# Ten of eleven FFN up products a block as seven half-size block products (Strassen form) in an fp32 two-block decoder kernel

## The chip, the cores and the metric

One Trainium2 chip (trn2), one of its cores. The metric is the device time of one execution in microseconds. All data and all matmuls are fp32.

## The reference, cut to what matters

Two blocks over x of 256 tokens x 1024 features: an mLSTM layer, a conv FFN, a shared key/value projection, an attention layer, a second conv FFN; then two more layers (convolution and sparse attention) that are modulated by vectors computed from `c_2` and `w_ada_2`. The change is in the conv FFN, which runs twice:

```python
def conv_ffn(x, norm_g, w_up, conv_w, conv_b, w_down):   # x 256 x 1024, w_up 1024 x 5632, w_down 2816 x 1024
    u = rmsnorm(x, norm_g) @ w_up
    up = jnp.pad(u, ((0, 0), (CONV_W - 1, 0), (0, 0)))
    c = conv_b + up[:, 0:s_] * conv_w[0]                 # CONV_W = 3 taps over the tokens
    for j in range(1, CONV_W):
        c = c + up[:, j:j + s_] * conv_w[j]
    val, gate = jnp.split(c, 2, axis=-1)
    return (jax.nn.silu(gate) * val) @ w_down
```

## The kernel before, in words

Everything is written out by hand for five engines, which meet through counting semaphores: `eng.wait_ge(S(name), n)` holds an engine, `.then_inc(S(name), n)` raises the count when the instruction is done. Each engine's instructions run in the order in which they stand, and so do the DMAs that SyncE (SP) issues.

The activations live transposed, features on the partitions: `hT`, `xg` and `sq` are 128 x 8 x 256 (8 chunks of 128 features, 256 tokens). A weight tile is 1 MB, 128 x 8 x 256: 256 output columns for all 1024 inputs. Outside the FFN such tiles go through `ring`, eight slots, with tile n in slot n % 8; SP's `load(n)` waits until the product that last used the slot is done.

An FFN (`ffn(f)` on each engine, f = 0 and 1) takes D_FF = 2816 in 11 steps of 256 value and 256 gate columns; g = 11 f + i counts the steps over both. Steps 0, 1 and 10 are written out, steps 2 to 9 are a hardware loop of four turns of two. `fring` has two buffers (par = parity of the step), each with the value and the gate tile of w_up and the tile of w_down.

- TensorE (`up`, L958 to L971; `down`, L973 to L986): up is 2 halves (value, gate) x 2 column chunks x 8 inner chunks = 32 matmuls of 128 x 128 weights against 256 tokens. An fp32 matmul is two MATMUL instructions in the trace, each with a weight load. The product goes to banks 4 and 5 or 6 and 7 by parity. The order is up(g), down(g - 1), up(g + 1), and so on. down is 16 matmuls that accumulate into banks 0 to 3 over all steps. up(g) waits for the copies of step g - 2, down(g) for `act_ready` of step g. In the block's first product the matmuls follow `xg_ready` chunk by chunk; the matmul that sums the squares for the norm (`ss`, L814) stands after it. xg is x times the norm's gain; the factor 1/rms is applied to the product, in the copy.
- VectorE (`step`, L1461): copies the product out of PSUM times 1/rms (L1464, two of 512 elements), adds taps 1 and 2 (L1478, eight of 256), in steps 2 to 9 folds one row chunk of w_ada into an accumulator in two halves of 1536 elements (L1493), and multiplies the gated value (L1500). The first tap waits for ScalarE's tap 0.
- ScalarE (L542 to L554): tap 0 with the bias (L549, four of 256), then silu (L553).
- SP (`ffn_loads`, L329): for each step of the loop first `load_ffn`, which issues the two w_up tiles (L313, after `up_done` of step g - 2), then the w_down tile (L317, after `down_done` of step g - 2), then `load_ada` with the two halves of w_ada (L325), each of which waits for `ada_free`, raised by the fold (L1493) of that half in the step before. `f_ada` has one buffer a half:

```python
sp.wait_ge(S("ada_free"), 2 * (8 * l + k) + half + 1)      # k = i - 2
```

So SP's order in the loop is: up g, down g, w_ada of g, up g + 1, down g + 1, w_ada of g + 1. Before and after the FFN's loads stand the ring loads: 8 to 23 ahead of the first FFN, 24 to 39 ahead of the second, and after the second the bias rows (L356, `skew`).

Ahead of each FFN stand four products (tiles 12 to 15, and 28 to 31) whose results VectorE adds to hT (`add_pair`, L1324).

Of the kernel before, what the change touches and what calls it, by code (L numbers as in the profile page):

```python
# [18 lines left out]
ALU = mybir.AluOpType  # L19
ACT = mybir.ActivationFunctionType  # L20
# [99 lines left out]
def model(nc, I, out):  # L120
    with ExitStack() as ctx:
# [31 lines left out]
        def W(a, b):  # L153
            return work[:, a:b]
# [46 lines left out]
        f_t = [three(W(7168 + 512 * i, 7680 + 512 * i), 2) for i in range(2)]  # L201
        f_u = W(8192, 8192 + 4 * 258).rearrange("p (g c t) -> p g c t", g=2, c=2)
        f_sg = W(9300, 9812)

        sqf = sq[:, :, :].rearrange("p a b -> p (a b)")
        sc_sb = [sqf[:, DIAG * i:DIAG * (i + 1)] for i in range(2)]
# [37 lines left out]
        def cut(w, c, n=256):  # L244

            return w.rearrange("(k p) n -> p k n", p=P)[:, :, c:c + n]

        def slot(n):
            return ring[:, n % RING, :]

        def slot8(n):
            return slot(n).rearrange("p (k n) -> p k n", k=8)
# [24 lines left out]
        ring_count = []  # L277
        for n, parts in enumerate(loads):
            landed[n % RING] += 16 * len(parts)
            ring_count.append(landed[n % RING])  # L280

        def arrived(eng, n):

            eng.wait_ge(S(f"ring{n % RING}"), ring_count[n])

        def product(eng, n):

            eng.wait_ge(S("product"), n + 1)
# [8 lines left out]
        @block.sync  # L297
        def _(sp):
            def load(n):
                if n >= RING:  # L300
                    product(sp, n - RING)
                for dst, src in loads[n]:
                    sp.dma_start(dst, src).then_inc(S(f"ring{n % RING}"), 16)

            def load_ffn(f, i, par, first):

# [47 lines left out]
            sp.wait_ge(S("rows_out"), 16)  # L354

# [36 lines left out]
        def _(act):  # L392
# [146 lines left out]


            def ffn(f):
                def step(g, i, par):  # L542
# [12 lines left out]

                g0 = FF_STEPS * f
                for i in (0, 1):
                    step(g0 + i, i, (g0 + i) % 2)
# [226 lines left out]
        def _(pe):  # L785
# [168 lines left out]
            def ffn(f, nth):  # L954

                g0 = FF_STEPS * f

                def up(g, par, turn, x_ready=None):  # L958

                    if x_ready is None:  # L960
                        pe.wait_ge(S("u_ready"), g - 1)
                    pe.wait_ge(S(f"f_up{par}"), 32 * turn)
                    for j in range(2):
                        w = fring[:, par, j, :].rearrange("p (k n) -> p k n", k=8)
                        for c in range(2):
                            for k in range(DC):
                                if x_ready is not None and j == 0 and c == 0:
                                    x_ready(k)
                                last = mm(pb[4 + 2 * par + j][:, T * c:T * (c + 1)], w[:, k, P * c:P * (c + 1)],  # L969
                                          xg[:, k, :], start=(k == 0), stop=(k == DC - 1))  # L970
                    last.then_inc(S("up_done"), 1)  # L971

                def down(g, par, turn, first=False, end=False):  # L973

                    pe.wait_ge(S(f"f_down{par}"), 16 * turn)
                    pe.wait_ge(S("act_ready"), g + 1)
                    w = fring[:, par, 2, :].rearrange("p (k n) -> p k n", k=2)
                    for k in range(2):
                        for m in range(DC):
                            last = mm(pb[m // 2][:, T * (m % 2):T * (m % 2 + 1)], w[:, k, P * m:P * (m + 1)],  # L980
                                      f_act[:, par, T * k:T * (k + 1)],
                                      start=(first and k == 0 and m % 2 == 0), stop=(end and k == 1),
                                      skip_group_check=True)
                            if end and k == 1 and m in (1, 3, 5):
                                last.then_inc(S("out_bank"), 1)
                    last.then_inc(S("down_done"), 1)  # L986

                p = g0 % 2
                up(g0, p, g0 // 2 + 1, x_ready=xg_ready(8 + 16 * f))
                ss(nth, pb[0][:, 0:T])  # L990
                up(g0 + 1, 1 - p, (g0 + 1) // 2 + 1, x_ready=lambda k: None)
                down(g0, p, g0 // 2 + 1, first=True)
                with pe.Fori(0, 4) as j:
                    for s in range(2):
                        g = 2 * j + (g0 + s + 2)
                        up(g, (g0 + s) % 2, j + ((g0 + s) // 2 + 2))
                        down(g - 1, (g0 + s + 1) % 2, j + ((g0 + s - 1) // 2 + 2))
                g = g0 + FF_STEPS - 1
                up(g, g % 2, g // 2 + 1)
# [263 lines left out]
        def _(dve):  # L1263
# [159 lines left out]
            for h in range(M_HEADS):  # L1423
# [31 lines left out]
            def ffn(f, nth, nn):  # L1455
                residual_norm(nth)
                g0 = FF_STEPS * f
                mean_square(nth, pb[0][:, 0:T], ms[:, 0:T], D)
                newton(nn, ms[:, 0:T], rbc, nwt[:, 0:T])

                def step(g, i, par, ada=None):  # L1461
                    dve.wait_ge(S("up_done"), g + 1)
                    for q in range(2):
                        ins = v.tensor_tensor(f_u[:, q, :, 2:2 + T], three(pb[4 + 2 * par + q][:, :], 2), rbc2,  # L1464
                                              ALU.mult)
                    ins.then_inc(S("u_ready"), 1)
                    dve.wait_ge(S("u_ready"), g + 1)
                    for tap in (1, 2):
                        marks = [] if tap == 1 else marks
# [40 lines left out]
                for i in (0, 1):  # L1510
                    step(g0 + i, i, (g0 + i) % 2)
                start = done[1]
                with dve.Fori(0, 4) as j:
                    per = 2 * 7
                    done[0] = per * j
                    for s in range(2):
                        i = 2 * j + s + 2
                        step(g0 + i, i, (g0 + s) % 2, ada=16 * (2 * j + s + 1))
                    assert done[1] - start == per
                done[0], done[1] = 0, start + 4 * per  # L1520
                i = FF_STEPS - 1
# [275 lines left out]
```

## Time and profile before

| | |
|---|---|
| median of 3 runs | 1095.95 us (1094.37 to 1096.34) |
| profiled execution, first to last instruction | 1092.9 us |
| mean granted TensorE clock | 0.987 |
| TensorE (PE) matmul busy | 1031.6 us, 94% |
| TensorE weight loads (PEld) busy | 886.1 us, 81% |
| VectorE (DVE) busy | 499.7 us, 46% |
| ScalarE (ACT) busy | 251.7 us, 23% |
| DMA | 168.12 MB, mean 154 GB/s |

The profile gives for the profiled execution its span, 1092.9 us; no further time of that execution is shown, so the runs' median stands beside it, 3.0 us higher. Times in the views count from the span's start. The first FFN runs from 156.6 to about 389 us, the second from 520.2 to about 752 us. Busy shares are averages over stages with different limits; in the FFN TensorE has no gap. The granted clock is a share of full speed (2.4 GHz); 0.5 is 1.2 GHz.

### The profile page before, as it was taken

The numbers are of one execution on the slowest core, as the hardware profiler recorded it, in microseconds if no ns is written. First come the engines' busy times: TensorE is split into PE (matmuls) and PEld (weight loads), VectorE is DVE, ScalarE is ACT, GpSimd is POOL, SyncE is SP. The second block draws the span as 40 slices with busy tenths as digits, with TensorE's granted clock in tenths as the row PEclk, the third lists the DMA queues.
The fourth block names the chain that finished last, engine by engine and source line by source line (L and its number), as shares of the span: only waits on it lengthen the run. The fifth ranks groups of instructions, "written<-read, shape, count | busy, mean of one in ns | idle before, by whom it ended". The sixth has DMA issues, their size and how long they took to land.

```text
span 1092.9 us, 12810 instructions
## 1 busy us (share of the span) xinstructions
PE 1031.6 (94%) x4887; PEld 886.1 (81%) x4887; DVE 499.7 (46%) x1160; ACT 251.7 (23%) x524; POOL 17.1 (2%) x23
## 2 busy tenths in 40 slices
PE   6999899999999999999999999998998896998987
PEld 5787688888888888888888888886886685887776
DVE  2301525334533543331435335336199944189951
ACT  1111202101101112351111011014223523233432
POOL 0000000000000000000000000000002000002000
PEclk9999999999999999999999999998999998999999
DMA  8993242676676454423346765732332054323001
GB/s 259 359 326 97 63 149 77 236 248 208 223 253 214 152 195 154 146 74 119 116 174 213 254 224 198 255 104 68 118 116 78 2 171 157 118 87 106 1 1 39
DMA packets 128832, 168.12 MB, mean 154 GB/s; under 512 B 7555, under 2 KB 116115, under 8 KB 128659
## 3 DMA queue, kind: packets, MB, share of 16 engines
q1 hardware_dynamic: 124592, 164.70, 45.6%
q10 hardware_dynamic: 4195, 2.81, 0.9%
q8 instruction: 29, 0.48, 0.2%
q14 instruction: 16, 0.13, 0.0%
HBM read 166.31 MB, written 1.06 MB: 153 GB/s over the span
## 4 chain that ended last, share of the span: by engine, by line
PE 77%; DVE 19%; ACT 2%; issue 1%; DMA 0%; ACTq 0%; DVEq 0%
PE bank L969 28%; PE bank L796 15%; PE bank L980 14%; DVE work L1657 8%; PE bank L807 8%; PE bank L1213 4%; PE bank L1127 1%; DVE fring L1679 1%; DVE sq L1594 1%; DVE fring L1692 1%; PE bank L1089 1%; PE bank L1245 1%; DVE fring L1688 1%; DVE sq L1585 1%; PE bank L814 1%
## 5 line engine op out<-in xcount | busy, mean ns | idle before, releaser
L969 PE MATMUL bank<-xg,fring 128*128 128x256 f32 x1408 | 307.6, 379 | 1.1 <-DVE xg L1307 1.1
L969 PEld LDWEIGHTS bank<-xg,fring 128*128 128x128 f32 x1408 | 267.4, 190 | 37.8 <-issue 1.5
L796 PE MATMUL bank<-xg,ring 128*128 128x256 f32 x960 | 218.5, 387 | 11.2 <-ACT xg L670 8.2
L796 PEld LDWEIGHTS bank<-xg,ring 128*128 128x128 f32 x960 | 185.3, 194 | 41.6 <-issue 9.9
L980 PE MATMUL bank<-work,fring 128*128 128x256 f32 x704 | 155.6, 379 | 0.0
L980 PEld LDWEIGHTS bank<-work,fring 128*128 128x128 f32 x704 | 133.4, 190 | 18.3 <-issue 0.3
L549 ACT ACTIVATE work<-work,cols 128x256 f32<-128x256 f32 x88 | 45.8, 592 | 291.2 <-DVE work L1464 291.2
L1464 DVE TENSOR_TENSOR work<-bank,rstd 128x512 f32<-128x512 f32 x44 | 28.4, 686 | 174.5 <-PE bank L969 174.5
L1657 DVE SCALAR_TENSOR_TENSOR work<-work,cols 128x256 f32<-128x256 f32 x240 | 98.5, 484 | 1.4 <-ACT work L709 1.3
L1478 DVE SCALAR_TENSOR_TENSOR work<-work,cols 128x256 f32<-128x256 f32 x176 | 71.6, 480 | 53.3 <-ACT work L549 53.3
L807 PE MATMUL bank<-ring,xg 128*128 128x256 f32 x320 | 69.9, 379 | 0.0
L807 PEld LDWEIGHTS bank<-ring,xg 128*128 128x128 f32 x320 | 60.6, 190 | 8.1
L1213 PE MATMUL bank<-ring,fring 128*128 128x256 f32 x256 | 57.1, 380 | 2.1 <-DVE fring L1720 2.1
L1493 DVE SCALAR_TENSOR_TENSOR work<-work,cact 128x1536 f32<-128x1536 f32 x32 | 58.1, 1816 | 0.6
L796 PE MATMUL bank<-work,ring 128*128 128x256 f32 x256 | 56.2, 379 | 0.5 <-ACT work L636 0.5
L1213 PEld LDWEIGHTS bank<-ring,fring 128*128 128x128 f32 x256 | 48.3, 190 | 10.0 <-issue 2.9
L796 PEld LDWEIGHTS bank<-work,ring 128*128 128x128 f32 x256 | 48.4, 190 | 7.1 <-ACT work L636 0.7
L1324 DVE TENSOR_TENSOR hT<-hT,bank 128x512 f32<-128x512 f32 x16 | 11.0, 687 | 58.1 <-PE bank L796 51.6
L622 ACT ACTIVATE sq<-sq,sml 128x128 f32<-128x128 f32 (+1 forms) x48 | 21.5, 449 | 46.7 <-DVE sml L1585 46.7
L406 ACT ACT_TABLE_LOAD x21 | 26.9, 1283 | 22.4 <-issue 22.0
L387 POOL TENSOR_TENSOR fring<-fring 128x384 f32<-128x384 f32 x16 | 16.1, 1012 | 1005.3 <-DVE fring L1696 959.4
L442 ACT ACTIVATE sq<-hT 128x512 f32<-128x512 f32 x24 | 14.8, 630 | 73.3 <-DVE hT L1324 68.8
(231 smaller groups left out, 761.5 us busy)
## 6 DMA issues: line engine op xcount, KB each, us to landing
fring<-in_f_w_up SPq DMA_DIRECT2D x44, 1024.0 KB, 10.2
work<-in_w_ada SPq DMA_DIRECT2D x32, 768.0 KB, 6.0
fring<-in_f_w_down SPq DMA_DIRECT2D x22, 1024.0 KB, 4.9
ring<-in_w_in SPq DMA_DIRECT2D x18, 1024.0 KB, 5.2
ring<-in_a_w_in SPq DMA_DIRECT2D x12, 1024.0 KB, 12.2
ring<-in_w_kv SPq DMA_DIRECT2D x8, 1024.0 KB, 5.5
ring<-in_w_out SPq DMA_DIRECT2D x8, 1024.0 KB, 5.2
ring<-in_a_w_out SPq DMA_DIRECT2D x4, 1024.0 KB, 11.2
```

The source lines that it names most:

```text
L406: act.preload_act_table_set(name)
L549: nc.scalar.activation(f_t[v][:, c, :], f_u[:, v, c, 0:T], ACT.Identity, bias=col(f"f_conv_b{f}", n), scale=col(f"f_conv_w{f}", n)).then_i ...
L622: nc.scalar.activation(p_sb[n % 2][:, x:y], sc_sb[n % 2][:, x:y], ACT.Exp, scale=-1.0, bias=sml[:, at:at + 1], accum_out=sml[:, at + 4:at ...
L796: last = mm(bank[:, T * c:T * (c + 1)], w[:, k, at + P * c:at + P * (c + 1)], x[:, k, :], start=(k == 0), stop=(k == nk - 1))
L807: last = mm(bank[:, T * b:T * (b + 1)], x[:, k, P * b:P * (b + 1)], slot8(n)[:, k, :], start=(k == 0), stop=(k == DC - 1))
L969: last = mm(pb[4 + 2 * par + j][:, T * c:T * (c + 1)], w[:, k, P * c:P * (c + 1)], xg[:, k, :], start=(k == 0), stop=(k == DC - 1))
L980: last = mm(pb[m // 2][:, T * (m % 2):T * (m % 2 + 1)], w[:, k, P * m:P * (m + 1)], f_act[:, par, T * k:T * (k + 1)], start=(first and k = ...
L1213: last = mm(bank[:, T * m:T * (m + 1)], y2[:, k, P * b:P * (b + 1)], slot8(load)[:, k, :], start=(half == 1 and m == 0 and k == 4), stop=( ...
L1464: ins = v.tensor_tensor(f_u[:, q, :, 2:2 + T], three(pb[4 + 2 * par + q][:, :], 2), rbc2, ALU.mult)
L1478: ins = v.scalar_tensor_tensor(f_t[q][:, c, :], f_u[:, q, c, tap:tap + T], col(f"f_conv_w{f}", 44 * tap + n), f_t[q][:, c, :], ALU.mult, A ...
L1493: ins = v.scalar_tensor_tensor(acc, f_ada[:, half, :], k, acc, ALU.mult, ALU.add)
L1657: marks[c] = link(v.scalar_tensor_tensor(b_y[:, c, :], b_a[:, c, tap:tap + T], col("conv_w_2", 124 * l + 4 * tap + c), b_y[:, c, :], ALU.m ...
```

## The change

Steps 1 to 10 of each FFN compute the up product as seven block products. With the inputs split in halves of 512 (inner) and the tokens in halves of 128, and value and gate tile as the two output halves, each block product is 4 inner chunks x 128 columns x 128 tokens; a step has two column chunks c, so 2 x 7 x 4 = 56 matmuls of 128 tokens in place of 32 of 256. Step 0 of each FFN stays as it was (`up_plain`), with the matmul of the norm's squares moved inside it.

- The sums of x blocks (`t_x`, four of 512 elements) are made once a block, from `x_s`, x times gain times 1/rms, which VectorE computes beforehand (eight of 256). `x_s` lies in ring slot 3.
- The sums of weight blocks (`s_forms`, four of 1024 elements, one of them in place in the gate tile) are made by VectorE in every step for the step after it. They lie in ring slots 0 to 2. `s_forms` waits until both w_up tiles of that step have landed.
- The products of chunk c lie in banks 4 + 2c and 5 + 2c, for every step the same. up(g) now waits for `s_ready` and for the copies of step g - 1.
- ScalarE copies the first product of each chunk out of PSUM (128 elements, two a step); VectorE adds up the seven products (`products_out`: for each chunk three adds of 256 elements and one of 128).
- While the FFN runs, ring slots 0 to 3 are not free. The ring's tiles are placed by `place(n)`; tiles 20 to 23 and 36 to 39 are loaded only after the last up product of the FFN ahead of them.
- `load_ffn`, `load_ada` and the loop of `ffn_loads` are unchanged.

```diff
+        def place(n):
+            if n < 12:
+                return n % RING
+            if n < 20:
+                return n % 4 + 4
+            if n < 28:
+                return n % 4
+            if n < 36:
+                return n % 4 + 4
+            return (n + 4) % RING
...
@@ SP
-            for n in range(8, 24):
+            for n in range(8, 20):
                 load(n)
             ffn_loads(0)
+            sp.wait_ge(S("up_done"), FF_STEPS)
+            for n in range(20, 24):
+                load(n)
             load_ffn(1, 0, 1, False)
             load_ffn(1, 1, 0, False)
-            for n in range(24, 40):
+            for n in range(24, 36):
                 load(n)
             ffn_loads(1)
+            sp.wait_ge(S("up_done"), 2 * FF_STEPS)
+            for n in range(36, 40):
+                load(n)
...
@@ ScalarE, step
+                    if not plain:
+                        for c in range(2):
+                            act.wait_ge(S("up_three"), 2 * (g - 1 - f) + c + 1)
+                            nc.scalar.activation(f_p1[c], pb[4 + 2 * c][:, 0:P], ACT.Copy).then_inc(S("p1_out"), 1)
...
@@ TensorE
+                def up(g, par, first=False):
+                    pe.wait_ge(S("s_ready"), g - f)
+                    val, gate = [fring[:, par, j, :].rearrange("p (k n) -> p k n", k=8) for j in range(2)]
+                    for c in range(2):
+                        if c == 1 or not first:
+                            pe.wait_ge(S("u_ready"), g)
+                        if first and c == 0:
+                            pe.wait_ge(S("x_s_ready"), f + 1)
+                        one, two = pb[4 + 2 * c], pb[5 + 2 * c]
+                        for bank, at, w, x in ((one, 0, val[:, 0:4], x_s[:, 0:4, 0:P]),
+                                               (one, 1, val[:, 4:8], x_s[:, 4:8, 0:P]),
+                                               (one, 2, s_2[par], t_x[1]),
+                                               (two, 0, s_1[par], t_x[0]),
+                                               (two, 1, gate[:, 0:4], t_x[2]),
+                                               (two, 2, s_last[par], x_s[:, 4:8, P:T]),
+                                               (two, 3, gate[:, 4:8], t_x[3])):
+                            if first and c == 0 and x is t_x[1]:
+                                pe.wait_ge(S("t_ready"), f + 1)
+                            for k in range(4):
+                                last = mm(bank[:, P * at:P * (at + 1)], w[:, k, P * c:P * (c + 1)], x[:, k, :],
+                                          start=(k == 0), stop=(k == 3))
+                            if bank is one and at == 2:
+                                last.then_inc(S("up_three"), 1)
+                        last.then_inc(S("up_chunk" if c == 0 else "up_done"), 1)
...
-                up(g0, p, g0 // 2 + 1, x_ready=xg_ready(8 + 16 * f))
-                ss(nth, pb[0][:, 0:T])
-                up(g0 + 1, 1 - p, (g0 + 1) // 2 + 1, x_ready=lambda k: None)
+                up_plain(g0, p, g0 // 2 + 1, xg_ready(8 + 16 * f), lambda: ss(nth, pb[0][:, 0:T]))
+                up(g0 + 1, 1 - p, first=True)
...
@@ VectorE
+            def s_forms(par, turn):
+                dve.wait_ge(S(f"f_up{par}"), 32 * turn)
+                val, gate = [fring[:, par, j, :].rearrange("p (k n) -> p k n", k=8) for j in range(2)]
+                n = link(v.tensor_tensor(s_1[par], gate[:, 0:4], gate[:, 4:8], ALU.add))
+                v.tensor_tensor(gate[:, 0:4], val[:, 0:4], gate[:, 0:4], ALU.subtract)
+                after(n)
+                n = link(v.tensor_tensor(s_2[par], s_1[par], val[:, 0:4], ALU.subtract))
+                after(n)
+                v.tensor_tensor(s_last[par], val[:, 4:8], s_2[par], ALU.subtract).then_inc(S("s_ready"), 1)
...
+            product(dve, 11)
+            s_forms(1, 1)
             for m in range(4):
                 product(dve, 12 + m)
...
+                for c in range(DC):
+                    ins = v.scalar_tensor_tensor(x_s[:, c, :], hT[:, c, :], col("f_norm", DC * f + c), rbc,
+                                                 ALU.mult, ALU.mult)
+                ins.then_inc(S("x_s_ready"), 1)
...
+                def products_out(g):
+                    for c in range(2):
+                        one, two = pb[4 + 2 * c], pb[5 + 2 * c]
+                        at = 8192 + 258 * c + 2
+                        dve.wait_ge(S("p1_out"), 2 * (g - 1 - f) + c + 1)
+                        n = link(v.tensor_tensor(spaced(at, f_quads[c] - at),
+                                                 f_p1[c].unsqueeze(1).broadcast_to([P, 2, P]),
+                                                 three(one[:, P:3 * P], 2), ALU.add))
+                        if c == 0:
+                            dve.wait_ge(S("up_chunk"), g - f)
+                        else:
+                            dve.wait_ge(S("up_done"), g + 1)
+                        after(n)
+                        then(v.tensor_tensor(f_u43[c], f_u2[c].unsqueeze(1).broadcast_to([P, 2, P]),
+                                             three(two[:, 0:2 * P], 2), ALU.add))
+                        v.tensor_tensor(spaced(at + P, 516 - P), f_u43[c], three(two[:, 2 * P:4 * P], 2), ALU.add)
+                        ins = v.tensor_tensor(f_u[:, 1, c, 2 + P:2 + T], f_u43[c][:, 1, :], two[:, 0:P], ALU.add)
+                    ins.then_inc(S("u_ready"), 1)
+
+                def step(g, i, par, ada=None, plain=False, turn=None):
+                    if turn is not None:
+                        s_forms(1 - par, turn)
+                    if plain:
+                        plain_out(g)
+                    else:
+                        products_out(g)
                     dve.wait_ge(S("u_ready"), g + 1)
...
+            product(dve, 27)
+            s_forms(0, 7)
```

## Rows read from the trace of the kernel before

**Rows 1.** Busy us (share of the span) and instructions of TensorE, from the page
```profile
PE 1031.6 (94%) x4887; PEld 886.1 (81%) x4887; DVE 499.7 (46%) x1160; ACT 251.7 (23%) x524; POOL 17.1 (2%) x23
```
**Rows 2.** The chain that ended last, in order of time: start us, us, what
```profile
156.55 14.05 PE bank L969 x64
...
191.79 13.81 PE bank L969 x64
...
212.51 13.81 PE bank L969 x64
...
357.55 13.81 PE bank L969 x64
```
**Rows 3.** Timeline of one step: start us, us, engine, line, what [idle before, releaser]
```profile
254.03 3.67 DVE L1493 SCALAR_TENSOR_TENSOR work<-work,cact 128x1536 f32<-128x1536 f32 x2
254.13 0.37 SPq L317 DMA_DIRECT2D fring<-in_f_w_down  x1
256.01 2.20 SPq L325 DMA_DIRECT2D work<-in_w_ada  x2
...
258.75 1.63 SPq L313 DMA_DIRECT2D fring<-in_f_w_up  x2
...
267.80 1.29 DVE L1464 TENSOR_TENSOR work<-bank,rstd 128x512 f32<-128x512 f32 x2 [9.22 <-PE bank L969]
269.26 2.08 ACT L549 ACTIVATE work<-work,cols 128x256 f32<-128x256 f32 x4 [15.27 <-DVE work L1464]
271.51 3.26 DVE L1478 SCALAR_TENSOR_TENSOR work<-work,cols 128x256 f32<-128x256 f32 x8 [2.42 <-ACT work L549]
...
274.68 3.67 DVE L1493 SCALAR_TENSOR_TENSOR work<-work,cact 128x1536 f32<-128x1536 f32 x2
```
**Rows 4.** What SP's queue waited for: us in total, times, longest us
```profile
SPq L317 <- PE bank L980: 302.8, 20, 19.8
...
SPq L325 <- DVE work L1493: 35.4, 28, 1.3
```
**Rows 5.** 128-column matmuls at full clock, L1245: timeline, then ns min/median/max
```profile
1085.97 1.39 PE L1245 MATMUL bank<-ms,work 128*128 128x128 f32 x11
...
L1245 PE MATMUL bank<-ms,work x9: 275/275/275, 1086.0 to 1086.9; 128*128 128x128 f32 x9
L1245 PEld LDWEIGHTS bank<-ms,work x9: 192/192/192, 1086.0 to 1086.9; 128*128 128x128 f32 x9
```
**Rows 6.** Groups of VectorE instructions by shape: count, busy us, mean ns, idle before
```profile
L1500 DVE TENSOR_TENSOR work<-work 128x512 f32<-128x512 f32 x22 | 15.2, 692 | 3.7 <-DVE work L1493 3.1
...
L1732 DVE SCALAR_TENSOR_TENSOR work<-bank,work 128x1024 f32<-128x1024 f32 x2 | 2.5, 1225 | 1.6 <-PE bank L814 1.6
...
L1382 DVE TENSOR_TENSOR work<-bank,consts 128x256 f32<-128x256 f32 x4 | 1.7, 422 | 1.0 <-PE bank L879 0.8
...
L1383 DVE TENSOR_TENSOR work<-bank,consts 128x128 f32<-128x128 f32 x4 | 1.1, 281 | 0.0
```
**Rows 7.** Issues of w_up tiles at 171.0 and at 258.8, us to landing
```profile
L313 SPq DMA_DIRECT2D fring<-in_f_w_up x2: 388/413/438, 171.0 to 171.5; - x2
DMA to landing us min/median/max: 5.3/6.4/7.6
...
L313 SPq DMA_DIRECT2D fring<-in_f_w_up x2: 383/718/1052, 258.8 to 259.3; - x2
DMA to landing us min/median/max: 8.9/10.0/11.1
```
**Rows 8.** Timeline at the first FFN's norm: sum of squares, inverse root
```profile
170.44 0.59 PE L814 MATMUL bank<-sq,ones 128*128 128x256 f32 x2
...
173.02 0.43 DVE L1292 SCALAR_TENSOR_TENSOR rstd<-nwt,rstd 128x256 f32<-128x256 f32 x1
```
**Rows 9.** Stretches: us, PE busy (count), mean granted clock, DMA share, GB/s
```profile
922.00:932.40 10.40, 5.02 (x11) 0.51 0.00 0
1082.40:1085.90 3.50, 3.50 (x19) 0.51 0.00 0
```

More of the change, by code:

```diff
@@ L203, in model, with spaced @@
         f_sg = W(9300, 9812)
+        f_quads = [9812 + 512 * c for c in range(2)]
+        f_u2 = [W(a, a + P) for a in f_quads]
+        f_u43 = [three(W(a + P, a + 3 * P), 2) for a in f_quads]
+        f_p1 = [W(a + 3 * P, a + 4 * P) for a in f_quads]
+        def spaced(at, step):
+            return three(W(at, at + 2 * step), 2)[:, :, 0:P]
         sqf = sq[:, :, :].rearrange("p a b -> p (a b)")
@@ L246, in cut @@
             return w.rearrange("(k p) n -> p k n", p=P)[:, :, c:c + n]
-        def slot(n):
-            return ring[:, n % RING, :]
+        def place(n):
[8 more added lines that the diff above has]
+            return (n + 4) % RING
+        def slot(n):
+            return ring[:, place(n), :]
+        s_sum = [ring[:, 0, 0:2048], ring[:, 1, 0:2048]]
+        s_last = [ring[:, 2, 1024 * i:1024 * i + 1024].rearrange("p (k n) -> p k n", k=4) for i in range(2)]
+        s_1 = [a[:, 0:1024].rearrange("p (k n) -> p k n", k=4) for a in s_sum]
+        s_2 = [a[:, 1024:2048].rearrange("p (k n) -> p k n", k=4) for a in s_sum]
+        x_s = ring[:, 3, :].rearrange("p (k n) -> p k n", k=DC)
+        t_x = [sq[:, 2 * i:2 * i + 2, :].rearrange("p a b -> p (a b)").rearrange("p (k n) -> p k n", k=4)
+               for i in range(4)]
         def slot8(n):
@@ L276, in model @@
         landed = [0] * RING
-        ring_count = []
+        holder = [None] * RING
+        ring_count, before = [], []
         for n, parts in enumerate(loads):
-            landed[n % RING] += 16 * len(parts)
-            ring_count.append(landed[n % RING])
+            landed[place(n)] += 16 * len(parts)
+            ring_count.append(landed[place(n)])
+            before.append(holder[place(n)])
+            holder[place(n)] = n
         def arrived(eng, n):
-            eng.wait_ge(S(f"ring{n % RING}"), ring_count[n])
+            eng.wait_ge(S(f"ring{place(n)}"), ring_count[n])
         def product(eng, n):
@@ L299, in load @@
             def load(n):
-                if n >= RING:
-                    product(sp, n - RING)
+                if before[n] is not None:
+                    product(sp, before[n])
                 for dst, src in loads[n]:
-                    sp.dma_start(dst, src).then_inc(S(f"ring{n % RING}"), 16)
+                    sp.dma_start(dst, src).then_inc(S(f"ring{place(n)}"), 16)
             def load_ffn(f, i, par, first):
@@ L541, in ffn, with step @@
             def ffn(f):
-                def step(g, i, par):
+                def step(g, i, par, plain=False):
+                    if not plain:
+                        for c in range(2):
+                            act.wait_ge(S("up_three"), 2 * (g - 1 - f) + c + 1)
+                            nc.scalar.activation(f_p1[c], pb[4 + 2 * c][:, 0:P], ACT.Copy).then_inc(S("p1_out"), 1)
                     act.wait_ge(S("u_ready"), g + 1)
@@ L557, in ffn @@
                 for i in (0, 1):
-                    step(g0 + i, i, (g0 + i) % 2)
+                    step(g0 + i, i, (g0 + i) % 2, plain=(i == 0))
                 with act.Fori(0, 4) as j:
@@ L956, in ffn, with up_plain @@
                 g0 = FF_STEPS * f
-                def up(g, par, turn, x_ready=None):
-                    if x_ready is None:
-                        pe.wait_ge(S("u_ready"), g - 1)
+                def up_plain(g, par, turn, x_ready, between):
                     pe.wait_ge(S(f"f_up{par}"), 32 * turn)
@@ L966, in up @@
                             for k in range(DC):
-                                if x_ready is not None and j == 0 and c == 0:
+                                if j == 0 and c == 0:
                                     x_ready(k)
-                                last = mm(pb[4 + 2 * par + j][:, T * c:T * (c + 1)], w[:, k, P * c:P * (c + 1)],
+                                if j == 0 and c == 1 and k == 4:
+                                    between()
+                                last = mm(pb[6 + j][:, T * c:T * (c + 1)], w[:, k, P * c:P * (c + 1)],
@@ L995, in ffn @@
                         g = 2 * j + (g0 + s + 2)
-                        up(g, (g0 + s) % 2, j + ((g0 + s) // 2 + 2))
+                        up(g, (g0 + s) % 2)
                         down(g - 1, (g0 + s + 1) % 2, j + ((g0 + s - 1) // 2 + 2))
                 g = g0 + FF_STEPS - 1
-                up(g, g % 2, g // 2 + 1)
+                up(g, g % 2)
                 down(g - 1, (g - 1) % 2, (g - 1) // 2 + 1)
@@ L1459, in ffn @@
                 newton(nn, ms[:, 0:T], rbc, nwt[:, 0:T])
-                def step(g, i, par, ada=None):
+                for c in range(DC):
+                    ins = v.scalar_tensor_tensor(x_s[:, c, :], hT[:, c, :], col("f_norm", DC * f + c), rbc,
+                                                 ALU.mult, ALU.mult)
+                ins.then_inc(S("x_s_ready"), 1)
+                dve.wait_ge(S("x_s_ready"), f + 1)
+                x11, x12, x21, x22 = x_s[:, 0:4, 0:P], x_s[:, 0:4, P:T], x_s[:, 4:8, 0:P], x_s[:, 4:8, P:T]
@@ L1462, in step, with plain_out @@
+                n = link(v.tensor_tensor(t_x[0], x12, x11, ALU.subtract))
+                v.tensor_tensor(t_x[2], x22, x12, ALU.subtract)
+                after(n)
+                then(v.tensor_tensor(t_x[1], x22, t_x[0], ALU.subtract))
+                v.tensor_tensor(t_x[3], x21, t_x[1], ALU.subtract).then_inc(S("t_ready"), 1)
+                def plain_out(g):
                     dve.wait_ge(S("up_done"), g + 1)
                     for q in range(2):
-                        ins = v.tensor_tensor(f_u[:, q, :, 2:2 + T], three(pb[4 + 2 * par + q][:, :], 2), rbc2,
-                                              ALU.mult)
+                        ins = v.tensor_tensor(f_u[:, q, :, 2:2 + T], three(pb[6 + q][:, :], 2), rbc2, ALU.mult)
@@ L1466, in step @@
                     ins.then_inc(S("u_ready"), 1)
+                def products_out(g):
[10 more added lines that the diff above has]
+                            dve.wait_ge(S("up_done"), g + 1)
+                        after(n)
+                        then(v.tensor_tensor(f_u43[c], f_u2[c].unsqueeze(1).broadcast_to([P, 2, P]),
[3 more added lines that the diff above has]
+                    ins.then_inc(S("u_ready"), 1)
@@ L1509, in ffn @@
                     dve.wait_ge(S("cact_done"), 1)
-                for i in (0, 1):
-                    step(g0 + i, i, (g0 + i) % 2)
+                step(g0, 0, g0 % 2, plain=True)
+                step(g0 + 1, 1, (g0 + 1) % 2, turn=(g0 + 2) // 2 + 1)
                 start = done[1]
                 with dve.Fori(0, 4) as j:
-                    per = 2 * 7
+                    per = 2 * 13
                     done[0] = per * j
@@ L1517, in ffn @@
                         i = 2 * j + s + 2
-                        step(g0 + i, i, (g0 + s) % 2, ada=16 * (2 * j + s + 1))
+                        step(g0 + i, i, (g0 + s) % 2, ada=16 * (2 * j + s + 1), turn=j + ((g0 + s + 3) // 2 + 1))
                     assert done[1] - start == per
```

## The prediction

> **What bounds the kernel now.** I read the page's busy times first: TensorE is busy for 94% of the span [rows 1], so the question is whether the change shortens TensorE's work, and what then keeps it fed. The chain in order of time shows the two FFN blocks as nothing but TensorE: an up product of 64 instructions in 13.81 us, then a down product in 6.91 us (212.51 - 191.79 - 13.81), 20.72 us from one step to the next [rows 2]. In the first block the up product of step 10 starts at 357.55, which is 201.0 us after the block's first one at 156.55; step 3's starts 55.96 us after it [rows 2]. The second block repeats the pattern.
>
> The timeline of one step shows the other engines waiting on TensorE [rows 3]. VectorE copies the product out (1.29 us from 267.80), ScalarE does tap 0 (2.08 us from 269.26), VectorE adds taps (3.26 us from 271.51) and then folds two pieces of w_ada (3.67 us from 274.68, ending 278.35). From the end of the copies (269.09) to that end it is 9.26 us. SP's queue hangs on this: it issues the first w_ada half at 256.01, when VectorE has ended the previous step's first fold (half of 3.67 after 254.03), the second half 1.85 us later, and only behind both, at 258.75, the up weights of the step after next. The view of SP's waits says so in totals: L325 waited 28 times for L1493, but at most 1.3 us at a time [rows 4]. Today this order is free, since nobody but TensorE reads those weights, and it does so 16 us after they are issued.
>
> **TensorE's part.** A step's up product is now 64 instructions (32 fp32 matmuls, two each) at 13.81/64 = 0.216 us. The new one has 2 column blocks x 7 products x 4 = 56 matmuls of 128 columns, 112 instructions, each with a weight load. The trace has 128-column fp32 matmuls with a new weight tile each, at full clock: 11 in 1.39 us, the last lasting 0.275, so (1.39 - 0.275)/10 = 0.112 us apart; as many loads stand beside them [rows 5]. So 112 x 0.112 = 12.5 us: 1.3 us less per step, not the eighth that seven products for eight suggest.
>
> Those loads last 192 ns each at 112 ns spacing, so loads and matmuls overlap though all use the full array. The Trainium skill (TensorE: Matmul & The Clock Gate, Part 3, The mechanism) says that a weight load overlaps a running matmul only where the row group differs. By that, each of the 112 would pay its load in full; the rows speak against it.
>
> **VectorE's part.** Its new step begins with the four weight sums, 128x1024 elements each. A two-input operation of that size takes 1.225 us, a plain one of 512 elements 0.692 us [rows 6]; the adds are taken at 1.225. Four of them, two chained by a wait, come to 5.0 us. The product copies (1.29 us) become, per column block, three adds of 256 elements (0.422 us) and one of 128 (0.281 us) [rows 6]: 1.55 us, 3.1 for both, 3.2 with the waits. Counted with its wait for ScalarE and the last multiply (0.69 us), VectorE's step rises from 1.3 + 9.3 + 0.7 = 11.3 us to 5.0 + 3.2 + 9.3 + 0.7 = 18.2 us. That alone would still fit beside TensorE's 12.5 + 6.9 = 19.4 us. ScalarE's two 128x128 copies fall while it is idle: nothing.
>
> **The wait that the change adds.** The sums of step g+1 stand in VectorE's queue ahead of the product copies of step g, and wait for the up weights of g+1 to land. SP issues these behind the w_ada pieces of step g, which wait until VectorE has folded those of step g-1. So VectorE waits for a load that its own last step released, and TensorE, whose banks are now single, waits for VectorE's copies before the next up product. Counted from the end of the copies of one step:
> - taps and folds to the end of the second fold: 9.26 us [rows 3]
> - first w_ada half issued 1.7 us before that end (256.01 against 257.70) [rows 3]
> - from its issue to the landing of the second up tile: 12.5 us, an estimate. Above: here it was 259.3 + 11.1 - 256.0 = 14.4 us with a down tile still in the queue [rows 3, 7]. Below: the second tile landed 7.6 us after its issue with nothing else under way [rows 7], and here it was issued 3.3 us after the first half (259.3 - 256.0) [rows 3, 7], so 10.9. The two tiles of 1 MB landed 2.8 us apart (7.6 + 0.5 - 5.3), which leaves 2.5 us ahead of the first one's data [rows 7]; 3.5 MB at that pace give 2.5 + 9.8 = 12.3, and with the fold's pause between the w_ada halves I take 12.5
> - sums 5.1 us with the start, copies 3.2 us
>
> Together 9.26 - 1.7 + 12.5 + 5.1 + 3.2 = **28.4 us a step** against 20.72. TensorE is done after 19.4 us and idles 9. The two ends of the load give 26.8 and 30.3.
>
> This ring holds where a load waits for a fold: for the up products of steps 4 to 10, seven periods. Before it: the plain product (14.05 us) and the sum of squares put step 1's product at 14.5 us after the block's start. The scaled x is wanted there: VectorE's inverse root stands 2.9 us after the sum of squares (170.44 to 173.45) [rows 8], and that now comes at 5.2 us; eight scalings at 0.4 us and four sums at 0.7 us bring it to 11.4 and 14.3. No wait. Step 1 ends at 27.0, down 0 at 33.9. SP then issues down 2, w_ada and up 3 together; such a set lands 16.3 us later (254.1 to 270.4) [rows 3, 7], at 50.3; sums and copies end at 58.6, where before the product of step 3 started at 55.96: +2.6 us. Seven periods: 7 x (28.4 - 20.72) = +53.8. The last up product is 1.3 us shorter. After each idle stretch TensorE's clock is at risk: the trace has 10.4 us and 3.5 us at a granted 0.51, the lower of the two levels, after TensorE waited [rows 9]. Inside the ring this is free (9 us of slack), but on the last up product it costs half of such a stretch, 1.8 to 5.2 us; I take 2.5, near the lower, since TensorE then works unbroken as at 1082. Per block 2.6 + 53.8 - 1.3 + 2.5 = 57.6, for two blocks +115.2 us.
>
> **Moves that cost nothing.** The first weight sums of each block (5 us) run beside a 6.9 us product ahead of the block. Ring tiles 20 to 23 and 36 to 39 are now loaded only at the last up product. Tile 20 is needed four token products later, some 40 us. Tiles 36 to 39 put 4 MB ahead of the bias transfer (L356): 2.5 + 5 x 2.8 = 16.5 us from the last up product's end to its landing, where TensorE asks for it after two down products and the transposes between, about 16 us. That is bare; a delay here would be 1 to 2 us, once, and is left at nothing.
>
> **Sum.** 1092.9 + 115.2 = 1208.1 us of span. The median of the runs, 1095.95, stands 3.0 us above the profiled span; with that, **1211 us**. By the two ends of the load (14 periods x -1.6 and +1.9) and of the clock (-1.4 and +5.4), the likeliest case spans 1187 to 1243.
>
> **Rivals.** (1) *Ring as above*: 0.82. (2) *The load never gates*, faster: the up weights are there when VectorE comes for them. Then TensorE's 19.4 us sets the step and 20 steps give 1.3 us each: 1095.95 - 26 = 1070 us. For it: each up tile lands well ahead of TensorE today, and L325's waits are short [rows 4]. Against: it decides at a ring below 19.4 us, so the landing would have to come 3.5 us after the first w_ada half's issue, and nothing lands so fast [rows 7]. 0.06. (3) *The clock stays low*: TensorE idles 9 of 28 us, the gate never opens, and both products take twice as long: 38.8 us a step, TensorE-bound, 1211 + 14 x 10.4 = 1357 us. Against: the low stretches in the rows end while TensorE works [rows 9]. 0.03. (4) *Loads don't overlap*: each new matmul waits for a load as long as its own 0.112 us, so the up product takes 112 x 0.224 = 25.1 us, the step 32.0 us, 14 x 3.6 more, and 12.6 more on the first and last such product of each block: 1211 + 50 + 50 = 1311 us. This is the case that the skill's rule gives; the spacing in the trace contradicts it [rows 5]. 0.02. (5) *A milder ring*: the load lands 5 to 10 us after the first w_ada half's issue, against the rows, and the period is 21 to 26 us: 1100 to 1180 us. 0.07.
>
> About 0.2% (2 us) is what a measurement of this kernel can tell from no change; only rival 2 lies below it. Faster 0.06, same 0.01, slower 0.93. The range is the likeliest case's own, with the top of rival 5 taken in: 1182 to 1243.
>
> **What would show it.** Right: VectorE idle some 12 us a step ahead of the first weight sum, ended by a DMA; TensorE idle some 9 us a step ahead of the new up product, ended by VectorE; steps 28.4 us apart from step 4 on, and up products of 12.5 us at full clock; SP's L325 waiting for L1493 for several us at a time; low clock digits inside both blocks. Wrong: up products back to back at 19.4 us, or TensorE busy through the block at a low clock.

## The result and the profile after

The changed kernel takes 1218.91 us (median of 4, 1217.7 to 1221.78) against 1096.14 us for the kernel before on the same chip: a ratio of 1.113, with a 95% interval of 1.111 to 1.115. It is 122.8 us slower. The forecast was 1211 us in a range of 1182 to 1243. The profiled execution has a span of 1220.0 us, 127.1 us over that of before. Of these, 3.9 us lie ahead of the first FFN, where the very first product ran longer (16.84 us against 14.05), before anything that the change touches; in the profiles of the six kernels below that product took from 14.05 to 16.94 us.

From the page of the changed kernel, busy times, then the slices of TensorE, its granted clock and the DMA:

```profile
PE 1049.7 (86%) x5847; PEld 931.6 (76%) x5847; DVE 634.5 (52%) x1384; ACT 260.6 (21%) x564; POOL 17.1 (1%) x23
...
PE   6999999767777799999987777787989889699887
...
PEclk9999899888888899999998888888999999799999
```

TensorE's share fell from 94% [rows 1] to 86%, and both FFN blocks can be seen as stretches of sixes, sevens and eights. Who waits for whom, from the view of waits (us in total, times, longest):

```profile
DVE ring L1391 <- DMA fring<-in_f_w_up: 178.3, 16, 12.3
PE bank L1034 <- DVE work L1575: 107.9, 16, 7.9
...
SPq L356 <- DVE work L1611: 205.6, 28, 14.7
```

Sixteen times VectorE waits at its first weight sum (L1391) for the up tiles, some 11 us each; sixteen times TensorE waits at the new up product (L1034) for VectorE's last copy. SP's wait for the fold grew from 35.4 us in 28 times [rows 4] to 205.6 us in the same 28. One step on the timeline (start us, us, engine, line, what, idle before it and what ended it):

```profile
239.99 1.22 DVE L1391 TENSOR_TENSOR ring<-fring 128x1024 f32<-128x1024 f32 x1 [12.27 <-DMA fring<-in_f_w_up]
241.13 1.22 DVE L1392 TENSOR_TENSOR fring<-fring 128x1024 f32<-128x1024 f32 x1
242.26 1.22 DVE L1394 TENSOR_TENSOR ring<-ring,fring 128x1024 f32<-128x1024 f32 x1
243.51 1.23 DVE L1396 TENSOR_TENSOR ring<-fring,ring 128x1024 f32<-128x1024 f32 x1
244.66 0.41 DVE L1564 TENSOR_TENSOR work<-work,bank 128x256 f32<-128x256 f32 x1
...
247.33 0.28 DVE L1575 TENSOR_TENSOR work<-work,bank 128x128 f32<-128x128 f32 x1
...
247.76 3.36 PE L1034 MATMUL bank<-ring,fring 128*128 128x128 f32 x16 [7.79 <-DVE work L1575]
247.79 2.07 ACT L590 ACTIVATE work<-work,cols 128x256 f32<-128x256 f32 x4 [17.99 <-DVE work L1575]
250.03 3.26 DVE L1596 SCALAR_TENSOR_TENSOR work<-work,cols 128x256 f32<-128x256 f32 x8 [2.42 <-ACT work L590]
...
253.21 3.67 DVE L1611 SCALAR_TENSOR_TENSOR work<-work,cact 128x1536 f32<-128x1536 f32 x2
...
255.18 2.20 SPq L356 DMA_DIRECT2D work<-in_w_ada  x2
...
257.58 1.31 SPq L344 DMA_DIRECT2D fring<-in_f_w_up  x2
...
261.68 7.07 PE L1047 MATMUL bank<-work,fring 128*128 128x256 f32 x32
268.73 1.23 DVE L1391 TENSOR_TENSOR ring<-fring 128x1024 f32<-128x1024 f32 x1 [10.97 <-DMA fring<-in_f_w_up]
```

Read it as a circle: sums from 239.99 (4.67 us), copies from 244.66 (to 247.61), tap 0, taps, folds (to 256.88). SP issues the first w_ada half at 255.18, the second at the end of the folds, the up tiles from 257.58. These land, and at 268.73 the next sums begin, 28.7 us after the last. Against [rows 3], where VectorE idled for TensorE (L1464), VectorE now idles for a load, and between TensorE's down product and its next up product there is a hole of 7.8 us.

The block's frame, from TensorE's timeline: step 1's product (two of its ten groups), and where those of steps 3 and 10 begin:

```profile
174.72 1.95 PE L1034 MATMUL bank<-ring,fring 128*128 128x128 f32 x16
...
186.33 1.06 PE L1034 MATMUL bank<-sq,fring 128*128 128x128 f32 x8
187.23 7.07 PE L1047 MATMUL bank<-work,fring 128*128 128x256 f32 x32
...
217.63 3.75 PE L1034 MATMUL bank<-ring,fring 128*128 128x128 f32 x16 [3.92 <-DVE work L1575]
...
420.24 3.76 PE L1034 MATMUL bank<-ring,fring 128*128 128x128 f32 x16 [6.46 <-DVE work L1575]
```

Step 1's product takes 187.23 - 174.72 = 12.5 us where 64 instructions took 13.81 [rows 2]. From step 3 to step 10 it is 202.6 us, 28.9 a step, where it was 145.0 [rows 2]. In the second block the same seven periods take 204.4 us (641.40 to 845.76). That is 57.6 and 59.3 us of the 127.1 in the span.

### The profile page after: what moved, and what is told of

It reads as the page before. It is cut to its first block, busy times and chain, and to the rows that moved or that the text cites. A ratio compares the mean times of both kernels' runs of the same rounds, so it can differ in the third digit from the quotient of the medians.

```text
span 1220.0 us, 15188 instructions
## 1 busy us (share of the span) xinstructions
PE 1049.7 (86%) x5847; PEld 931.6 (76%) x5847; DVE 634.5 (52%) x1384; ACT 260.6 (21%) x564; POOL 17.1 (1%) x23
## 4 chain that ended last, share of the span: by engine, by line
PE 42%; DVE 28%; DMA 16%; issue 8%; ACT 4%; SPq 1%; DVEq 1%; ACTq 0%
DMA fring<-in_f_w_up 14%; PE bank L837 14%; DVE work L1777 8%; PE bank L848 7%; PE bank L1034 5%; DVE work L1611 4%; PE bank L1279 3%; PE bank L1047 3%; PE bank L1010 2%; DVE work L1596 2%; ACT work L590 2%; DVE ring L1394 2%; PE bank L1193 1%; DVE work L1572 1%; DVE fring L1799 1%
## 5 line engine op out<-in xcount | busy, mean ns | idle before, releaser
L837 PE MATMUL bank<-xg,ring 128*128 128x256 f32 x960 | 222.2, 392 | 10.9 <-ACT xg L711 8.2
L837 PEld LDWEIGHTS bank<-xg,ring 128*128 128x128 f32 x960 | 188.2, 197 | 42.2 <-issue 10.0
L1034 PE MATMUL bank<-ring,fring 128*128 128x128 f32 x640 | 106.5, 336 | 107.9 <-DVE work L1575 107.9
L1034 PEld LDWEIGHTS bank<-ring,fring 128*128 128x128 f32 x640 | 100.6, 247 | 114.3 <-issue 65.1
L1391 DVE TENSOR_TENSOR ring<-fring 128x1024 f32<-128x1024 f32 x20 | 24.5, 1224 | 178.3 <-DMA fring<-in_f_w_up 178.3
L1034 PE MATMUL bank<-sq,ring 128*128 128x128 f32 x640 | 88.2, 297 | 0.0
L1034 PEld LDWEIGHTS bank<-sq,ring 128*128 128x128 f32 x640 | 86.3, 217 | 0.0
L1034 PE MATMUL bank<-sq,fring 128*128 128x128 f32 x640 | 84.5, 275 | 0.0
L1034 PEld LDWEIGHTS bank<-sq,fring 128*128 128x128 f32 x640 | 77.9, 192 | 0.0
L1279 PEld LDWEIGHTS bank<-ring,fring 128*128 128x128 f32 x256 | 48.3, 190 | 10.0 <-issue 2.9
L1034 PE MATMUL bank<-ring 128*128 128x128 f32 x320 | 42.3, 275 | 0.0
```

The costliest lines, as they stand in the source:

```text
L837: last = mm(bank[:, T * c:T * (c + 1)], w[:, k, at + P * c:at + P * (c + 1)], x[:, k, :], start=(k == 0), stop=(k == nk - 1))
L1034: last = mm(bank[:, P * at:P * (at + 1)], w[:, k, P * c:P * (c + 1)], x[:, k, :], start=(k == 0), stop=(k == 3))
L1279: last = mm(bank[:, T * m:T * (m + 1)], y2[:, k, P * b:P * (b + 1)], slot8(load)[:, k, :], start=(half == 1 and m == 0 and k == 4), stop=( ...
L1391: n = link(v.tensor_tensor(s_1[par], gate[:, 0:4], gate[:, 4:8], ALU.add))
```

## The experiments

Two kinds of reason were put against each other: the ring (VectorE's sums wait for a load that its own last fold released), and reasons that need no wait for a load: V, VectorE's added work; B, TensorE waiting for copies because its banks are single. The kernel before took 1096.62 us beside runs 1, 4, 5 and 6, and 1096.05 us beside runs 2 and 3.

**1. The order of the loads.** Under the changed kernel SP issues the up tiles of step g + 1 ahead of w_down and w_ada of step g (`load_up` and `load_down` are the two parts of `load_ffn`):

```diff
 def ffn_loads(f):
     sp.wait_ge(S("up_done"), FF_STEPS * f + 1)
+    load_up(f, 2, FF_STEPS * f % 2, False)
     with sp.Fori(0, 4) as j:
         for s in range(2):
-            load_ffn(f, 2 * j + s + 2, (FF_STEPS * f + s) % 2, False)
+            load_up(f, 2 * j + s + 3, (FF_STEPS * f + s + 1) % 2, False)
+            load_down(f, 2 * j + s + 2, (FF_STEPS * f + s) % 2, False)
             load_ada(f, 2 * j + s)
-    load_ffn(f, FF_STEPS - 1, (FF_STEPS * f + FF_STEPS - 1) % 2, False)
+    load_down(f, FF_STEPS - 1, (FF_STEPS * f + FF_STEPS - 1) % 2, False)
```

> The changed kernel, with one thing moved on SP's queue: the two w_up tiles of step g + 1 are issued ahead of w_down and w_ada of step g, as soon as the up product of step g - 1 is done. No engine's work changes. Theory (the ring: VectorE's sums wait for a load that VectorE's own last fold released): the ring is cut, the tiles land some 9 to 11 us after the up product two steps earlier, VectorE has them 5 us before it asks, and TensorE sets the step with 12.5 + 6.9 = 19.4 us. 14 periods x 9.6 us and twice some 2 us for a clock that stays up: 1219 - 139 = about 1075 us (1068 to 1085), under the kernel before. Rival V (VectorE's work of a step, 18 us with its wait for ScalarE, is what is late) and rival B (TensorE waits for copies because its banks are single): the order of loads does nothing for either, 1219 us.

Measured: 1071.13 us (median of 5), ratio to the kernel before 0.977, interval 0.976 to 0.979. Its chain in order of time in the middle of the first block, then the timeline of VectorE there:

```profile
251.46 12.50 PE bank L1045 x112
263.96 6.91 PE bank L1058 x32
270.87 12.51 PE bank L1045 x112
283.38 6.91 PE bank L1058 x32
```

```profile
255.28 0.69 DVE L1629 TENSOR_TENSOR work<-work 128x512 f32<-128x512 f32 x1 [0.19 <-DVE work L1622]
255.89 1.22 DVE L1402 TENSOR_TENSOR ring<-fring 128x1024 f32<-128x1024 f32 x1
...
264.09 0.42 DVE L1583 TENSOR_TENSOR work<-work,bank 128x256 f32<-128x256 f32 x1 [1.68 <-PE bank L1045]
```

TensorE has no gap, 19.41 us a step. VectorE goes from its last multiply into the sums (L1402) with no wait for the tiles and then idles for TensorE, not the other way round. Moving the issue of the two tiles is worth 148 us. V and B would have left 1219 us, and fall. This kernel is also faster than the one before, by 25.5 us, which is 20 x 1.3.

**2. The same order without VectorE's reads.** The same edit under the kernel before, with the full product.

> The kernel before, with the two w_up tiles of step g + 1 issued ahead of w_down and w_ada of step g, as in the run with that order under the changed kernel; the full product stays. Theory (the ring needs VectorE's wait on w_up): nobody but TensorE reads those tiles here and it does so late, so the order is worth nothing: 1096 us, within 3. Rival O (the order of the loads is itself worth time, whatever the product): faster than 1096 by several us.

Measured: 1096.04 us against 1096.05, ratio 1.000, interval 0.999 to 1.001. The order is worth nothing until VectorE reads the tiles; it is the pair that costs.

**3. Only the wait.** Under the kernel before:

```diff
 def step(g, i, par, ada=None, turn=None):
+    if turn is not None:
+        dve.wait_ge(S(f"f_up{1 - par}"), 32 * turn)
     dve.wait_ge(S("up_done"), g + 1)
```

> The kernel before, with nothing added but the wait: in steps 1 to 9 VectorE waits until the w_up tiles of the next step have landed before it copies the product out. No sums, full products, two pairs of banks. Theory (the ring): VectorE's step turns into 9.3 - 1.7 + 13.5 + 0.1 + 1.3 = 22.5 us between folds in place of 20.7, though it has less than 12 us of work. TensorE has some 9 us of slack against VectorE here (down of a step comes a whole up product later), so it feels only the end: a lag of 2.3 us at step 3 and 7 x 1.8 us after it, less 9.2, is some 5.5 us a block: about 1107 us (1100 to 1112). Rival V (work, not the wait): 1096 us and folds 20.7 us apart.

Measured: 1117.39 us, ratio 1.020, interval 1.018 to 1.022. Its VectorE timeline:

```profile
255.52 1.29 DVE L1466 TENSOR_TENSOR work<-bank,rstd 128x512 f32<-128x512 f32 x2 [11.79 <-DMA fring<-in_f_w_up]
...
277.78 1.29 DVE L1466 TENSOR_TENSOR work<-bank,rstd 128x512 f32<-128x512 f32 x2 [10.77 <-DMA fring<-in_f_w_up]
...
301.32 1.29 DVE L1466 TENSOR_TENSOR work<-bank,rstd 128x512 f32<-128x512 f32 x2 [12.12 <-DMA fring<-in_f_w_up]
```

The copies are 22.3 and 23.5 us apart, where TensorE alone would set 20.7. So a wait with no work behind it slows a kernel in which VectorE is half idle. I missed the size, 21 us for 11: TensorE reads the same tiles, which in the ring come late for it too (its waits for the up tiles are 14.1 us in 8 times, and two of the products after them took 15.7 us for 14.0). Some periods are also a microsecond longer than my 22.5; why was not tried.

**4. Sums behind the copies.** The changed kernel with the two calls in VectorE's step exchanged:

```diff
-    if turn is not None:
-        s_forms(1 - par, turn)
     if plain:
         plain_out(g)
     else:
         products_out(g)
+    if turn is not None:
+        s_forms(1 - par, turn)
```

> The changed kernel, with VectorE making the weight sums of step g + 1 behind the product copies of step g in place of ahead of them. The work is the same. Theory (the ring): the copies (2.95 us) no longer lie between the landing and the next fold; what is left of the ring is fold, load (13.5 us from the first w_ada half's issue), sums 4.8 us, ScalarE's tap 0, taps, fold: 28.9 - 2.95 = 26.0 us a step, 14 x -2.95 = -41, about 1178 us. Rival V: the same work, no change, 1219. Rival B: TensorE now waits for the sums behind the copies as well, 4.8 us more a step: slower than 1219.

Measured: 1132.59 us, ratio to the kernel before 1.034, interval 1.032 to 1.036: 86 us less, twice what I expected. From its timeline and its waits:

```profile
275.89 2.07 ACT L590 ACTIVATE work<-work,cols 128x256 f32<-128x256 f32 x4 [4.64 <-DVE work L1575]
278.90 1.23 DVE L1391 TENSOR_TENSOR ring<-fring 128x1024 f32<-128x1024 f32 x1 [3.20 <-DMA fring<-in_f_w_up]
...
283.58 3.25 DVE L1596 SCALAR_TENSOR_TENSOR work<-work,cols 128x256 f32<-128x256 f32 x8
```

```profile
DVE ring L1391 <- DMA fring<-in_f_w_up: 52.3, 16, 5.2
```

Copies and ScalarE's tap 0 are both over before the tiles land, so 2.95 and 2.4 us leave the ring, not 2.95 alone: 28.9 - 5.4 = 23.5 us, and the up products from step 3 on start 22.7 to 23.7 us apart in the first block. The 14 periods give 79 us of the 86; step 3's product, which begins 3.6 and 2.9 us earlier in its block than in the changed kernel, gives the rest. The ring is still there, shorter. V would have left 1219 us, since the work is the same, and B would have had this kernel slower than 1219, since TensorE waits for more; both fall again.

**5. More bytes ahead of the tiles.** The changed kernel, in `load_ada` (`extra` is a spare array in HBM):

```diff
+    sp.dma_start(extra[l].rearrange("k p n -> p k n")[:, bass.ds(k, 1), :],
+                 src[:, bass.ds(k, 1), 0:1536]).then_inc(S("extra_in"), 16)
```

> The changed kernel with one more transfer of 0.75 MB a step (a piece of w_ada to a spare array in HBM, read by nobody) issued between the w_ada halves and the w_up tiles of the next step. Theory (the ring): the tiles land 2.5 to 3.4 us later, every period of the ring is that much longer, and step 3 too: 16 x 3 = 48, about 1267 us (1255 to 1275). Rivals V and B: nobody on the path waits for it, 1219 us.

Measured: 1249.03 us, ratio 1.141, interval 1.139 to 1.144: 30.1 us more where I expected 48. The issue rows of the one step say why (first w_ada half, then the up tiles; us to landing):

```profile
L357 SPq DMA_DIRECT2D work<-in_w_ada x1: 346/346/346, 286.7 to 286.7; - x1
...
L345 SPq DMA_DIRECT2D fring<-in_f_w_up x2: 393/1127/1861, 290.3 to 290.9; - x2
DMA to landing us min/median/max: 8.9/10.0/11.1
```

The second tile lands 290.9 + 11.1 - 286.7 = 15.3 us after the first half's issue, 1.8 later than in the changed kernel (13.5), not 3. Over all 16 such loads the means are 15.6 and 13.9 us, and 16 x 1.7 = 27 of the 30.1 us: what the load is late by, the kernel is late by, in the main.

**6. The work without the wait.** In the changed kernel the sums are made from `xg` (all zeros), four operations of the same size, and TensorE takes over the wait for the tiles. The real weight sums are left out.

```diff
 def s_forms(par, turn):
-    dve.wait_ge(S(f"f_up{par}"), 32 * turn)
-    val, gate = [fring[:, par, j, :].rearrange("p (k n) -> p k n", k=8) for j in range(2)]
+    one, two = xg[:, 0:4, :], xg[:, 4:8, :]
... (the four operations read one and two)
-def up(g, par, first=False):
+def up(g, par, turn, first=False):
+    pe.wait_ge(S(f"f_up{par}"), 32 * turn)
     pe.wait_ge(S("s_ready"), g - f)
...
```

> The changed kernel with the weight sums made from xg in place of w_up (four operations of the same size, all zeros), so that VectorE does all of its new work but waits for no load; TensorE waits for the w_up tiles itself. It leaves out the real weight sums. SP's order is that of the changed kernel, so loads still hang on the folds. Theory (the ring): with the wait off VectorE's queue the chain from a fold over the load, the up product and the copies to the fold two steps on is 11.8 + 12.5 + 3.0 + 9.3 = 36.6 us for two steps, 18.3 a step, under TensorE's 19.4: about 1075 us, like the kernel with the loads reordered. Rival V: all of VectorE's work is still there, so 1219. Rival B: banks and copies are as they were, 1219.

Measured: 1070.18 us (ratio 0.978, interval 0.975 to 0.980), with SP's order that of the changed kernel. In its middle the chain is TensorE alone:

```profile
249.35 12.50 PE bank L1035 x112
261.86 6.91 PE bank L1048 x32
268.77 12.51 PE bank L1035 x112
```

All of VectorE's 18 us of work and the single banks are there and cost nothing. Together with run 1: take away either the load's place in the queue or VectorE's wait for it, and the whole 148 us go.

## Why the prediction was right, point by point

**TensorE's part.** 112 x 0.112 = 12.5 us stood for the product; step 1's took 12.5, and runs 1 and 6 turned 20 x 1.3 us into 25.5 and 26.4 us of whole time. That holds at full clock, in steps 1 and 2; after a wait the product took longer (below). The rule of the Trainium skill that the prediction weighed (TensorE: Matmul & The Clock Gate, Part 3, The mechanism), that a weight load overlaps a running matmul only across row groups, does not hold here: all 112 loads are of the full array, 190 to 192 ns each in step 1, and the product took 112 ns an instruction. Rival 4, which stood for it, was also priced too low by its own rows: with the 192 ns load in full a product would be 112 x (0.112 + 0.192) = 34.0 us, and the kernel, by estimate, about 1470 us, not 1311.

**VectorE's part.** Sums 4.67 us for 5.1, copies 2.95 for 3.2: I had added waits that the engine hides. (Ahead of the ring, the 2.9 us from 170.44 to 173.45 are 3.0.)

**The wait.** It lies where it was put, between the same two instructions, and is worth what the circle says. Term by term for the period from 239.99 to 268.73: sums 4.67, copies 2.95, to the end of the folds 9.26 (9.26 forecast), first half issued 1.7 before it (1.7), load 13.5 (12.5). Sum 28.7, forecast 28.4, and on average 28.9 and 29.2 in the two blocks, since the load took 13.2 to 14.8 us, 13.8 on average. **The load is the term that was mis-sized**, by 1.3 us a step. Sums and copies together were 0.7 us too long in the forecast (8.3 for 7.6), so half of that miss cancelled; that the step came out so close is partly luck. The issues of that step in the changed kernel, first and second w_ada half, then the two up tiles, each with its us to landing:

```profile
L356 SPq DMA_DIRECT2D work<-in_w_ada x1: 345/345/345, 255.2 to 255.2; - x1
DMA to landing us min/median/max: 4.4/4.4/4.4
...
L356 SPq DMA_DIRECT2D work<-in_w_ada x1: 345/345/345, 257.0 to 257.0; - x1
DMA to landing us min/median/max: 5.9/5.9/5.9
...
L344 SPq DMA_DIRECT2D fring<-in_f_w_up x2: 384/562/740, 257.6 to 258.1; - x2
DMA to landing us min/median/max: 8.4/9.5/10.6
```

The halves land at 259.6 and 262.9, the tiles at 266.0 and 268.7. The first half's 4.4 us are near the 2.5 + 2.1 = 4.6 of the forecast, the tiles' 3.1 and 2.7 near its 2.8. It is the second half that was mis-sized: 3.3 us behind the first, 3.1 to 4.4 in the 14 steps of the ring, where I had 2.1 and 0.2 for the pause between the issues. That need not be the transfer itself: in step 2 of the same kernel, where SP issues the halves 0.6 us apart, just behind a w_down tile, they land 1.9 us apart, at 202.0 and 203.9:

```profile
L356 SPq DMA_DIRECT2D work<-in_w_ada x1: 346/346/346, 195.1 to 195.1; - x1
DMA to landing us min/median/max: 6.9/6.9/6.9
...
L356 SPq DMA_DIRECT2D work<-in_w_ada x1: 345/345/345, 195.7 to 195.7; - x1
DMA to landing us min/median/max: 8.2/8.2/8.2
```

In the ring the second half is issued 1.85 us after the first, once its fold is done, and nothing is queued ahead of the two. Which of these makes the difference no run shows, since none changed one alone. The trace of before gave no single value either: there, always with a w_down tile ahead, the halves land 1.9 to 4.2 us apart.

**Ahead of the ring** step 3's product began 57.2 us after the block's first (217.63 - 160.40), for 58.6; the scaled x caused no wait. **The last product** of the block took 14.7 us (420.24 to 434.92), 0.9 over before, in the second block 1.4 over; -1.3 + 2.5 = +1.2 was forecast. **The moves** that were costed at nothing: the bias transfer's bare cover did not hold. TensorE waited for it once, 1.91 us:

```profile
879.50 3.70 PE L1178 MATMUL bank<-fring,consts 128*128 128x512 f32 x8 [1.91 <-DMA fring<-bias_rows]
```

From the end of the last w_down product to the end of the span it is 343.3 us for 342.6, so 0.7 us of it is left. Per block the profile has 1.3 + 57.6 + 0.9 = 59.8 and 1.9 + 59.3 + 1.4 = 62.6 for a forecast of 57.6; the remaining 4.7 us are the 3.9 ahead of the first block, the 0.7 of the bias rows and rounding.

**The rivals.** That the load never gates (1070 us) is what both runs that cut the ring show as its price: the sum for it was right, its condition absent. The clock came back while TensorE worked, so the ring was never TensorE's. A milder ring is what run 4 made, though with less of VectorE's work in it, not with a faster load (13.7 us there). **The signs.** VectorE idled 11.1 us a step ahead of its sums for a forecast of 12. In the ring TensorE idled 6.1 to 7.9 us, 7.1 on average, for a forecast of 9, since the products that follow ran partly at the lower clock: 13.9 to 15.5 us for 12.5. The sign of up products of 12.5 us at full clock held only ahead of the ring, and the clock digits inside the blocks fell, but only to 8.

## What to carry to other kernels

When an engine is made to read an operand that only TensorE read before, the operand's load gets a new deadline, often a step earlier: follow the load back through its queue to what each transfer ahead of it waits for. If that is the same engine's own work, the two form a ring, whose period is the sum of the work, the issue and the landing, however idle the engines look. Ask for the order of issues before asking for less work: here moving two issues ahead of a transfer that waits turned +11% into -2.3%.

## What the runs showed of the hardware

After each wait in the ring (6.1 to 7.9 us) TensorE began its product at the lower clock. From stretches of the changed kernel (us, PE and PEld busy, DVE, ACT, POOL busy, mean granted clock, DMA share, GB/s):

```profile
217.60:221.00 3.40, 3.37 (x16) 3.40 (x17) 1.00 (x3) 2.07 (x4) 0.00 (x0) 0.50 0.16 66
...
247.70:251.00 3.30, 3.24 (x17) 3.27 (x18) 0.97 (x3) 2.07 (x4) 0.00 (x0) 0.57 0.00 0
251.00:254.00 3.00, 3.00 (x30) 3.00 (x29) 3.00 (x7) 0.80 (x2) 0.00 (x0) 1.00 0.00 0
```

At 1.2 GHz the first 16 instructions of a product take 3.4 to 3.8 us where they take 2.0 at 2.4 GHz, and each product in the ring takes 13.9 to 15.5 us for 12.5. In the ring that fell into TensorE's own slack; only the block's last product paid for it, 2.2 and 2.7 us.

The second thing: how far apart two transfers of 0.75 MB land was no fixed number. In the changed kernel the second w_ada half landed 1.9 us after the first where it was issued 0.6 us behind it and a w_down tile stood ahead (both blocks), and 3.1 to 4.4 us after it where it was issued 1.85 us behind and nothing stood ahead. In the kernel before, the two pairs issued 0.6 us apart landed 3.3 and 1.9 us apart. In run 5 the extra 0.75 MB, from HBM to HBM, was issued right behind the second half (at 289.2), landed 1.8 us after it (at 296.2), and the tiles came 1.7 us later on average; whether a transfer into SBUF would have cost the same was not tried.
